# A value tile as the first tile of a hybrid decoder block's kernel: its place, the turns of x around it, and the decay sums a third earlier

## What is computed

```python
h = rms_norm(x, norm_pre_w)
proj = jnp.einsum('bsd,df->bsf', h, w_in)          # all projections at once
qkv_a, z_a, beta_a, dec_a, qkv_b, z_b, gate_logits = jnp.split(proj, cuts, axis=-1)
qkv_a = silu(causal_depthwise_conv(qkv_a, conv_w))  # four taps; q, k, v of mixer a
g = -exp(dn_a_log) * softplus(dec_a + dn_dt_bias)   # log decays, 8 heads
oa = gated_delta_rule(qa, ka, va, g, beta)          # cumulated g, decay = exp(gdiff), triangular solve
ob = moba_attention(qb, kb, vb, rel_bias)           # softmax attention with a relative bias
merged = gates[:, :, 0] * (ya @ w_branch[0]) + gates[:, :, 1] * (yb @ w_branch[1])
return x + rms_norm(merged @ w_out, norm_post_w)
```

## Time and profile before

| | us |
|---|---|
| median of three timed runs | 354.43 |
| lowest and highest of them | 354.10, 355.68 |
| the profiled execution | 355.41 |
| its span | 353.6 |
| PE busy in the span | 345.3 |
| DVE busy | 269.3 |
| ACT busy | 220.8 |
| POOL busy | 59.9 |

### The profile page before, as it was taken

How to read it: one execution, slowest core, us unless ns; L and a number is a source line. 1 busy time by engine, 2 the same in 40 slices (tenths; PEclk the granted TensorE clock), 3 DMA queues, 4 the chain that set the end, 5 groups by cost and what they waited for, 6 DMA issues and landing times.

```text
span 353.6 us, 7456 instructions
## 1 busy us (share of the span) xinstructions
PE 345.3 (98%) x2753; PEld 331.9 (94%) x2753; DVE 269.3 (76%) x565; ACT 220.8 (62%) x499; POOL 59.9 (17%) x112
## 2 busy tenths in 40 slices
PE   8999999999999999999999999999999999999993
PEld 5899988999999999999999999999999999999882
DVE  3969697499996868978789787887977557688644
ACT  5778696355456667686876868677677655444421
POOL 1533526510033000300203011030200201000011
PEclk9999999999999999999999999999999999999998
DMA  7958948897799574555656465655555555775813
GB/s 227 274 151 188 322 113 210 227 285 171 202 253 224 154 179 120 152 150 137 161 138 161 126 169 130 168 133 139 154 155 146 162 169 170 216 239 189 250 38 119
DMA packets 100321, 62.48 MB, mean 177 GB/s; under 512 B 4692, under 2 KB 95230, under 8 KB 100286
## 3 DMA queue, kind: packets, MB, share of 16 engines
q1 hardware_dynamic: 98030, 58.59, 60.7%
q0 software_dynamic: 1072, 3.04, 3.1%
q10 hardware_dynamic: 1184, 0.39, 0.5%
HBM read 60.41 MB, written 1.59 MB: 175 GB/s over the span
## 4 chain that ended last, share of the span: by engine, by line
PE 87%; DMA 4%; DVE 3%; issue 2%; POOL 1%; ACT 1%; SPq 1%; DVEq 0%; POOLq 0%; ACTq 0%
PE banks L1347 63%; PE banks L1560 6%; PE banks L1365 4%; DMA th_E<-g_rows 2%; DMA g_rows<-grow 1%; DVE w_lo L890 1%; PE banks L1445 1%; PE banks L1462 1%; PE banks L1451 1%; DMA relb<-in_rel_bias_dram 1%; PE banks L1332 1%; POOL th_E L500 1%; DVE acc L974 1%; PE banks L1291 1%; PE banks L1512 1%
## 5 line engine op out<-in xcount | busy, mean ns | idle before, releaser
L890 DVE TENSOR_TENSOR w_lo<-raw,w_hi 128x1024 fp32r<-128x1024 f32 x102 | 124.1, 1219 | 45.0 <-ACT w_hi L637 44.4
L637 ACT CAST w_hi<-raw 128x1024 fp32r<-128x1024 f32 x103 | 107.6, 1048 | 10.3 <-PE banks L1560 5.5
L1347 PE MATMUL banks<-h_hi,w_hi 128*128 128x256 f32 x568 | 81.3, 286 | 0.0
L1347 PE MATMUL banks<-h_lo,w_hi 128*128 128x256 f32 x568 | 76.6, 277 | 0.0
L1347 PE MATMUL banks<-h_hi,w_lo 128*128 128x256 f32 x568 | 76.4, 277 | 0.0
L1347 PEld LDWEIGHTS banks<-h_hi,w_hi 128*128 128x128 f32 x568 | 71.0, 189 | 0.3
L1347 PEld LDWEIGHTS banks<-h_lo,w_hi 128*128 128x128 f32 x568 | 69.9, 188 | 0.0
L1347 PEld LDWEIGHTS banks<-h_hi,w_lo 128*128 128x128 f32 x568 | 69.9, 188 | 0.0
L974 DVE SCALAR_TENSOR_TENSOR acc<-banks,vec,acc 128x255 f32<-128x255 f32 (+2 forms) x72 | 34.5, 480 | 5.8 <-ACT acc L692 2.3
L587 POOL TENSOR_TENSOR so<-so,rnq 128x2 f32<-128x2 f32 x8 | 2.6, 330 | 162.8 <-ACT junk L828 162.8
L761 ACT ACTIVATE acc<-banks,vec 128x256 f32<-128x256 f32 x16 | 7.6, 475 | 18.6 <-PE banks L1347 18.6
(11 more groups left out here) (243 smaller groups left out, 546.5 us busy)
## 6 DMA issues: line engine op xcount, KB each, us to landing
raw<-in_w_in_dram SPq DMA_DIRECT2D x79, 512.0 KB, 4.1
raw<-in_w_branch_dram SPq DMA_DIRECT2D x16, 512.0 KB, 3.7
raw<-in_w_out_dram SPq DMA_DIRECT2D x8, 512.0 KB, 3.3
xin<-in_x_dram SPq DMA_DIRECT2D x2, 512.0 KB, 3.7
th_E<-g_rows POOLq DMA_DIRECT2D x2, 512.0 KB, 7.7
bias<-bias_rows POOLq DMA_DIRECT2D x1, 1024.0 KB, 7.5
raw<-in_x_dram SPq DMA_DIRECT2D x2, 512.0 KB, 4.4
out_dram<-xin SPq DMA_DIRECT2D x4, 256.0 KB, 2.0
```

The source lines that it names most:

```text
L637: nc.scalar.copy(w_hi[:, t % SLOTS, :], raw[:, t % SLOTS, :]).then_inc(s_hi, 1)
L890: v.tensor_tensor(w_lo[:, t % SLOTS, cols], raw[:, t % SLOTS, cols], w_hi[:, t % SLOTS, cols].bitcast(F32), ALU.subtract).then_inc(s_lo, 1)
L1347: last = mm(ps, w, r, start=part == 0 and k == 0, stop=part == 2 and k == KT - 1)
```

## The change

The first tile becomes a value tile, and the first key tile the second (`FIRST`); all others stay. With it:

- The first tile's two halves are two blocks of 128 rows by 512 columns. POOL subtracts each half as soon as that half is cast, where it waited for both.
- `x_T` uses five banks, 1, 2, 3, 5 and 0, since the values need banks 6 and 7 from the start. Ten turns stand ahead of the first product instead of twelve, six between the products instead of four.
- `first_tile` is written anew: 12 products of 512 columns for blocks 0 and 1 of h, with the turns of blocks 5, 6 and 7 between them.
- ACT casts tile 1 after block 5 of h, not after block 7. DVE makes the remainder of `wbd` ahead of both halves of tile 1's remainder, not between them.
- The key tile's products wait for each block of h by itself (n == 1 in `third`), and its first for the block that lay in bank 0.
- The decay sums stand at S = 11 instead of 12, on PE and on DVE. The turn of key 0 stands at S = 12 instead of 10.

```diff
-FIRST = "KVKKVKKVKKVKVVVV"
+FIRST = "VKKKVKKVKKVKVVVV"
...
-TOKENS = {10: 0, 16: 1, 19: 2, 24: 3, 27: 4, 32: 5, 35: 6, 41: 7}
+TOKENS = {12: 0, 16: 1, 19: 2, 24: 3, 27: 4, 32: 5, 35: 6, 41: 7}
...
-        x_T = [bank[(1, 2, 3, 5, 6, 7)[k % 6]][:, SEQ * (k // 6):SEQ * (k // 6) + SEQ] for k in range(KT)]
+        x_T = [bank[(1, 2, 3, 5, 0)[k % 5]][:, SEQ * (k // 5):SEQ * (k // 5) + SEQ] for k in range(KT)]
...
             for half in range(2):
-                part = slice(KT // 2 * half, KT // 2 * half + KT // 2)
-                sp.dma_start(raw[:, 0, :].rearrange("p (k n) -> p k n", k=KT)[:, part], w_tile(COL_K)[:, part]
+                sp.dma_start(raw[:, 0, 512 * half:512 * half + 512], w_in[P * half:P * half + P, COL_VB:COL_VB + 512]
                              ).then_inc((s_w0_in, s_raw[0])[half], 16)
...
-            pool.wait_ge(s_hi, 1)
             for half in range(2):
                 cols = slice(D // 2 * half, D // 2 * half + D // 2)
+                pool.wait_ge((s_w0_hi, s_hi)[half], 1)
...
                 ac(h_hi[:, k, :], x_T[k], ACT.Copy, scale=vec[:, R_PRE + k:R_PRE + k + 1]).then_inc(s_h_hi, 1)
-            sa.wait_ge(s_hi, 1)
-            split_hi(1, 1, 1)
+                if k == 5:
+                    sa.wait_ge(s_hi, 1)
+                    split_hi(1, 1, 1)
...
-            ve.wait_ge(s_lo, 2)
-            first_lo(1, 0, s_lo)
             ve.wait_ge(s_bd_hi, 1)
             v.tensor_tensor(wbd2[:, :, 2 * HEADS:], wbd[:], wbd2[:, :, 0:2 * HEADS].bitcast(F32),
                             ALU.subtract).then_inc(s_bd_s, 1)
+            ve.wait_ge(s_lo, 2)
+            first_lo(1, 0, s_lo)
...
-                elif S == 12:
+                elif S == 11:
                     ve.wait_ge(s_gc_p, 1)
...
             pe.wait_ge(s_pre_xb[0], 1)
-            pe.wait_ge(s_vec, 1)
-            for k in range(4, 6):
-                turn(0, k)
+            turn(0, 4)
...
             pe.wait_ge(s_pre_xb[1], 1)
-            for k in range(4, 6):
-                turn(1, k)
+            turn(1, 4)
...
-                elif S == 12:
+                elif S == 11:
 
                     pe.wait_ge(s_g, 2)
...
             def first_tile():
 
...
+                def first_turn(k):
+
+                    pe.wait_ge(s_h_lo, k - 4)
+                    for c in range(NC):
+                        turn(c, k)
+
+                def first_products(kk, left, right):
+
+                    for c in range(NC):
+                        mm((bE, bF)[c], left[:, kk, P * c:P * c + P], right[:, 0, 512 * kk:512 * kk + 512],
+                           start=kk == 0 and left is h_hi and right is w_hi, stop=False)
+
+                pe.wait_ge(s_vec, 1)
                 pe.wait_ge(s_w0_hi, 1)
...
+                pe.wait_ge(s_h_hi, 1)
+                first_products(0, h_hi, w_hi)
+                first_turn(5)
+                first_products(0, h_lo, w_hi)
+                pe.wait_ge(s_hi, 1)
+                pe.wait_ge(s_h_hi, 2)
+                first_products(1, h_hi, w_hi)
+                first_turn(6)
+                first_products(1, h_lo, w_hi)
+                first_turn(7)
+                pe.wait_ge(s_lo, 1)
+                first_products(0, h_hi, w_lo)
+                pe.wait_ge(s_lo, 2)
+                for c in range(NC):
+                    last = mm((bE, bF)[c], h_hi[:, 1, P * c:P * c + P], w_lo[:, 0, 512:], start=False, stop=False)
                 last.then_inc(s_tile, 1)
...
                 for k in range(KT):
+                    if n == 1 and part < 2:
+                        pe.wait_ge((s_h_hi, s_h_lo)[part], k + 1)
...
                     j = K_TILES.index(n)
+                    if j == 0:
+                        pe.wait_ge(s_h_lo, 5)
                     if j >= 2:
                         pe.wait_ge(s_tap, 3 * (j - 1))
```

More of the change, by code:

```diff
@@ L1311, in first_tile @@
             def first_tile():
-                ps = bank[0][:, 0:SEQ]
-                order = ("hh0 hh1 lh0 hh2 lh1 hh3 lh2 hl0 hh4 lh3 hl1 hh5 lh4 hl2 hh6 lh5 hl3 hh7 lh6 hl4 "
-                         "hl5 hl6 hl7 lh7").split()
-                pe.wait_ge(s_w0_hi, 1)
-                for i, which in enumerate(order):
-                    k = int(which[2])
-                    if which == "hh4":
-                        pe.wait_ge(s_hi, 1)
-                    if which in ("lh0", "lh1"):
-                        pe.wait_ge(s_h_lo, k + 1)
-                        for c in range(NC):
-                            turn(c, 6 + k)
-                    if which[0] == "l":
-                        pe.wait_ge(s_h_lo, k + 1)
-                    else:
-                        pe.wait_ge(s_h_hi, k + 1)
-                    if which[1] == "l":
-                        pe.wait_ge(s_lo, 1 + k // 4)
-                    last = mm(ps, (w_lo if which[1] == "l" else w_hi)[:, 0, P * k:P * k + P],
-                              (h_lo if which[0] == "l" else h_hi)[:, k, :], start=i == 0, stop=i == 23)
+                def first_turn(k):
[7 more added lines that the diff above has]
+                pe.wait_ge(s_vec, 1)
+                pe.wait_ge(s_w0_hi, 1)
+                pe.wait_ge(s_h_hi, 1)
[13 more added lines that the diff above has]
+                    last = mm((bE, bF)[c], h_hi[:, 1, P * c:P * c + P], w_lo[:, 0, 512:], start=False, stop=False)
                 last.then_inc(s_tile, 1)
```

## The result

The changed kernel takes 355.46 us (median of 21 runs, 355.13 to 356.06), the kernel before 354.41 (21 runs beside it, 354.05 to 355.84): a ratio of 1.0023, 95% interval 1.0013 to 1.0033, or about 1 us slower. The forecast was 353.8, in a range of 352.6 to 355.0. The profiled execution took 355.43 us with a span of 353.6, just what the profiled one of before took.

What follows compares the result with a forecast made beforehand. From 51 us PE's products bound the kernel; before that, the chain through `grow`, store, broadcast and mask to the decays. Operands gain 0.7 us, taken as 0.65: 355.41 becomes 354.8 profiled, 353.8 as median; range 352.6 to 355.0.

Steps and rivals of the forecast that it cites:

- the head start on PE: At the start: the value tile ends at 12.1 and not 13.13, so PE reaches the second tile a microsecond sooner.
- The first step that failed: Tile 3's load lands unchanged, so ACT's gate-sum copy still starts at 16.90 and takes 0.5 us of PE's microsecond.
- The wait at the copy: PE waits for ACT's copy of the gate sums (line 662) till 17.35; 0.5 us of its microsecond is lost.
- `grow`: DVE's step towards the decays: starts at 26.4 instead of 27.11, 0.7 us gained on the decays.
- PE's wait for `tab`: In tile 3: PE asks for the gates' last step a third sooner and waits 0.8 us, till 23.4.
- the tap: DVE's third tap of key 0 ends at 20.7, so PE starts tile 3 there, waiting about 0.25 us.
- the first decay: On ACT, behind store, broadcast and mask: starts at 40.75 instead of 41.47, shifted by 0.7 us.
- the second rival: Weight load issued at 31.2 takes 9.7 us, first decay 0.4 late: 354.8; chance 0.18, shared with decays no sooner.
- The second step that failed: The sum starts from the profiled run's 355.41 us, 0.98 above the median 354.43, and the difference carries over.
- Both holes: PE's waits for operands at 44.65 and 50.89, worth 0.83 and 0.36 us; first gone, second small afterwards.
- the decays' gain: Decay operands reach PE 0.7 us sooner; taken as -0.65 us on the whole time.

Runs made afterwards that it cites:

- the old shapes: Changed kernel with its first two loads in the kernel before's run lengths (1024 runs of 512 bytes, then 256 of 2048): 354.41 us, ratio 0.9997.
- a run without holes: Kernel before, unedited, profiled again on a run of 354.07 us, span 352.2; PE shows no wait from 42 us on.

## Why the prediction was wrong

- **Right: the head start on PE.** From the first product to the second tile PE took 3.56 us (8.95 to 12.51) where 3.40 was reckoned (8.70 to 12.1) and before took 4.35 and 4.38, so the gain is 0.8 us and not a whole one.
- **The first step that failed, 1.05 us:** "nothing in the change makes that load smaller or puts fewer bytes ahead of it. So the copy still starts at 16.90". The bytes are the same, but the order of the run lengths isn't: the key tile's 1024 short runs now come second, with only a load of constants between them and the 1024 of `wbd`. SP's hang, which had fallen on tile 3's own issue, falls on that of `alog`, which lasts 2.38 us and not 0.58. Tiles 2 and 3 are issued at 9.75 and 10.23 instead of 8.0 and 8.5 and tile 3 lands 0.92 us later. The wait at the copy, reckoned as half a microsecond of the head start, took all of it and more: the turn came at 18.23, not 17.35. The swap of run lengths, in both directions, the small loads put later and `wbd` in another queue show it. The prediction had looked at when loads land, not at how long SP takes to issue them, though the trace of before had the sign: the 2.28 us of tile 3's issue. With the old shapes in the changed kernel the chain comes out as reckoned: the copy at 16.80 (16.90 reckoned), PE's turn at 17.20 (17.35), tile 4 at 25.36 (25.46), `grow` at 26.30 (26.4).
- **Right, but 0.9 us later:** PE's wait for `tab` (0.68 us by pace, 0.8 reckoned), the tap (tile 2 took 3.11 us instead of 2.93), and `grow`, 27.31 and not 26.4. All hang on the copy.
- **Right by luck:** the first decay at 40.44 (40.75 reckoned), since the store of `g_rows` took 1.9 us from issue to the next step and not 3.87. What the first decay followed was not the decays at all: the mask behind the broadcast was done by 38.8, and the decay came right behind ACT's cast of tile 10 at 39.49. The load of that tile, which the second rival would have had late, was issued at 32.1 and landed after 7.1 us, between the two bounds of the earlier trace rows; by the rule of the Trainium skill ("DMA: Bandwidth & Descriptors", section "Queues, rings and completion order") quoted in the prediction it would be late, and it was. ACT was busy up to that cast, so nothing was lost.
- **The second step that failed, 0.6 us:** "I make the sum against the profiled run and carry the difference over to the median". Both holes closed, as forecast, but the holes, 1.2 us by pace, are what the usual run doesn't have; the three times shown (354.10, 354.43, 355.68) had the two levels in them. The changed kernel with the old shapes, where the chain is as reckoned, took 354.41, just what the kernel before takes (354.46 beside it). Carrying over took 0.98 us off the 354.8; that kernel makes 0.4 of it good, since its first decay came at 39.65 and PE has no reported wait behind the one for `tab`, and 0.6 stays. A sum against a run without holes would have had only PE's start to go by: 0.8 us of head start, less the waits for the copy, the tap and `tab`.

The two steps together are the miss: 355.46 measured, 353.8 forecast, of which 1.05 is the stall (355.46 against 354.41, on two chips) and 0.6 the base. The changed kernel shows one level, 355.13 to 356.06, and the decays' gain doesn't show against the lower level of the kernel before.

## What to carry to other kernels

When a change permutes loads, look at the issue times in the queue that carries them as well as at the landing times: equal bytes in another order of run lengths can move the load at which the issuing engine hangs, and all the loads behind it are late. So have behind it what is wanted last. Ask of the profile which of the timed runs it is: a gain on waits that only some of the runs have is worth only their share. A step taken off one wait (the sums moved back) mostly meets the next operand in line, so cost the next one too before counting the gain.

## What was not expected of the hardware

SP hangs at the issue of one load while many short runs stand ahead in its queue, in each of the kernels whose loads are told above, for 1.7 to 3.4 us; which load it is depends on the order. While it hung at `alog` in after, from 6.86 to 9.24 us, the DMA engines were busy; they fell nearly idle behind it, when tiles 2 and 3 had only just been issued (9.75 and 10.23). Windows of one microsecond of after (window, its length, busy time and count of PE, PEld, DVE, ACT, POOL, then PE's granted clock, DMA share, GB/s):

```profile
7.00:8.00 1.00, 1.00 (x8) 0.62 (x7) 0.75 (x3) 0.64 (x1) 0.33 (x1) 1.00 0.94 207
8.00:9.00 1.00, 0.72 (x8) 0.51 (x6) 0.26 (x2) 0.75 (x3) 0.74 (x1) 1.00 1.00 281
...
11.00:12.00 1.00, 1.00 (x7) 0.82 (x6) 0.78 (x2) 1.00 (x2) 0.94 (x2) 1.00 0.17 22
12.00:13.00 1.00, 1.00 (x8) 0.88 (x8) 0.70 (x2) 0.82 (x3) 1.00 (x1) 1.00 0.48 77
```

In the kernel before the shares of the last two are 0.36 and 1.11. How many runs the queue holds no run here shows.

PE also shows two paces at the same granted clock of 1.00. Without holes, the kernel before keeps 0.91 us for eight products; after goes at 0.94 to 0.95 from a wait of 0.2 us at 33.32 on, until past 40 us. Timeline of PE, first the kernel before without holes, then after, then the kernel before with both sums at S = 11:

```profile
38.13 1.07 PE L1347 MATMUL banks<-h_lo,w_hi 128*128 128x256 f32 x8
39.04 1.07 PE L1347 MATMUL banks<-h_hi,w_lo 128*128 128x256 f32 x8
```

```profile
33.32 0.41 PE L1420 MATMUL banks<-cst,kT_all 128*128 128x128 f32 x2
...
39.42 1.11 PE L1354 MATMUL banks<-h_lo,w_hi 128*128 128x256 f32 x8
40.37 1.11 PE L1354 MATMUL banks<-h_hi,w_lo 128*128 128x256 f32 x8
```

```profile
30.50 1.11 PE L1347 MATMUL banks<-h_hi,w_lo 128*128 128x256 f32 x8
31.44 1.11 PE L1347 MATMUL banks<-h_hi,w_hi 128*128 128x256 f32 x8
```

The profile of before with holes does the same from 32.16 on. But a wait is not what brings the slower pace: the third of these kernels goes at 0.94 from 28.39 on without one ahead of it, and the changed kernel with PE's sums at S = 12 goes faster, at 0.90 instead of 0.95, behind one at 33.76. In after it makes some 0.2 us between tiles 4 and 10 (0.45 us longer than in the run without holes, 0.21 of it the wait at 33.32); what it comes from was not tried, and stays open. Nor was it settled what puts a run of the kernel before at one level or the other: in the two profiles the first decay differs by 2.3 us.
